# Two-block kernel: recurrent results kept on chip, adaLN in 1024-column steps, five taps on other engines, channel norm between tiles

## The reference

```python
h = rmsnorm(x, norm_g) * (1 + scale) + shift
cv, cg, cs, lx, ls = split(h @ w_in)                  # 5 x 1024 channels
v = cv * sigmoid(cg)
v = causal_depthwise_conv(v, dw_w, dw_b)              # 31 taps
v = silu(layernorm(v, cln_g, cln_b))                  # over channels
y_conv = (v @ pw2_w + pw2_b) * silu(cs)
xs = causal_depthwise_conv(lx, sc_w, sc_b)            # 4 taps
r, i = sigmoid(xs @ wr + br), sigmoid(xs @ wi + bi)   # 8 heads of 128
a = exp(-8 * r * softplus(-lam))
hs = linear_scan(a, sqrt(1 - a * a) * i * xs)         # along tokens
y_lru = hs * silu(ls)
x = x + (1 + gate) * (concat(y_conv, y_lru) @ w_out); x = rmsnorm(x, final_g)
# second block
mods_x, mods_ctx = silu(c_2) @ ada_w + ada_b, silu(c_ctx) @ ada_w + ada_b
# mLSTM mixer in both directions over a context of 256 and the 1024 tokens, then a gated conv-FFN
```

## Time and profile before

| | us |
|---|---|
| median of 3 runs | 2440.98 |
| the three runs | 2440.98, 2437.72, 2441.24 |
| the profiled execution, its own time | 2437.03 |
| its span in the trace | 2435.2 |
| TensorE matmul busy | 2170.7 (89%) |
| DVE busy | 1205.0 (49%) |
| ACT busy | 722.6 (30%) |
| POOL busy | 660.5 (27%) |

### The profile page before, as it was taken

The page is one execution under the profiler, slowest core; times in us unless marked ns, Lnnn a source line. Parts: engine busy times, 40 slices in busy tenths (PEclk is TensorE's granted clock), DMA queues, the critical chain, the costliest instruction groups (busy, mean ns, idle before and its releaser), DMA issues.

```text
span 2435.2 us, 25833 instructions
## 1 busy us (share of the span) xinstructions
PE 2170.7 (89%) x9824; PEld 1791.3 (74%) x9824; DVE 1205.0 (49%) x1196; ACT 722.6 (30%) x827; POOL 660.5 (27%) x300
## 2 busy tenths in 40 slices
PE   3599999995889997999997994978999999999995
PEld 3488777774667775788886993846888888887874
DVE  6699989998563436603305654045222222222124
...
GB/s 302 152 52 52 37 117 97 117 72 62 113 52 69 121 78 18 162 81 201 214 100 259 225 157 233 43 95 27 51 43 69 78 64 65 78 61 113 74 56 69
DMA packets 290235, 251.43 MB, mean 103 GB/s; under 512 B 7091, under 2 KB 262676, under 8 KB 290164
## 3 DMA queue, kind: packets, MB, share of 16 engines
...
## 4 chain that ended last, share of the span: by engine, by line
PE 51%; issue 32%; POOL 6%; DVE 5%; DMA 4%; ACT 2%; SPq 0%; ACTq 0%; POOLq 0%; DVEq 0%
PE PS L1277 40%; POOL wl L667 4%; PE PS L1519 1%; PE PS L1511 1%; PE PS L1512 1%; DVE SCR L1623 1%; PE PS L1545 1%; PE PS L1397 1%; PE PS L1299 1%; DMA B<-rows_d 1%; DMA B<-in_mod_w 1%; DMA SCR<-lru_d 1%; PE PS L1485 1%; PE PS L1505 1%; DMA SCR<-in_ctx 1%
## 5 line engine op out<-in xcount | busy, mean ns | idle before, releaser
L1277 PE MATMUL PS<-XH,wh 128*128 128x512 f32 x2416 | 753.0, 393 | 34.3 <-POOL wl L667 25.2
L1277 PE MATMUL PS<-XH,wl 128*128 128x512 f32 x2416 | 748.7, 391 | 0.0
L1277 PE MATMUL PS<-XL,wh 128*128 128x512 f32 x2416 | 748.6, 391 | 0.0
L667 POOL TENSOR_TENSOR wl<-raw,wh 128x1024 fp32r<-128x1024 f32 (+2 forms) x173 | 409.0, 2364 | 1214.0 <-ACT wh L851 1044.4
L1277 PEld LDWEIGHTS PS<-XH,wh 128*128 128x128 f32 x2416 | 454.5, 189 | 135.1 <-issue 19.8
L1277 PEld LDWEIGHTS PS<-XH,wl 128*128 128x128 f32 x2416 | 456.7, 189 | 96.2
L1277 PEld LDWEIGHTS PS<-XL,wh 128*128 128x128 f32 x2416 | 456.2, 189 | 95.7
L1709 DVE SCALAR_TENSOR_TENSOR PS<-B,PJ,PS 128x1022 f32<-128x1022 f32 (+28 forms) x232 | 295.1, 1272 | 8.2 <-DVE SC L1765 0.2
L851 ACT ACTIVATE wh<-raw 128x1024 fp32r<-128x1024 f32 (+1 forms) x124 | 129.5, 1045 | 309.2 <-PE PS L1277 223.1
L2073 DVE SCALAR_TENSOR_TENSOR SCR<-SCR,PV 128x1008 f32<-128x1008 f32 x22 | 28.0, 1271 | 256.6 <-ACT SCR L1213 256.6
L914 ACT ACTIVATE wh<-raw 128x1024 fp32r<-128x1024 f32 (+1 forms) x48 | 45.6, 950 | 237.0 <-PE PS L1277 205.1
(11 more groups left out here) (304 smaller groups left out, 2440.6 us busy)
## 6 DMA issues: line engine op xcount, KB each, us to landing
...
```

Source lines behind the costliest of these rows:

```text
L667: tt(wl[slot][:, 0:kc, :], raw[slot][:, 0:kc, :], wh[slot][:, 0:kc, :].bitcast(F32), ALU.subtract).then_inc(lo_done, 1)
L1277: last = mm(ps[:, c:c + step_n], W[:, k, :], Y[:, k, c:c + step_n], start=(seen == 0), stop=(seen == total - 1))
```

## The change

Recurrent results: step i writes its product to a buffer of its own (`lru_out[i]`), and nothing goes to DRAM or back. After its last taps DVE splits the first five, high and low, then forms the eighth; ACT rounds the last three, DVE subtracts for all. The output product is one of eight tiles (G1). Its first two tiles run in the order: tile one chunks 1 to 7, tile two chunks 1 to 4, tile one chunk 8, tile two chunks 5 to 8. In the eighth step the gate product stands before the cs tile, and ACT makes the filter's high part before it empties ls. The cs tile frees the input's chunks one by one.

adaLN: 16 + 32 row tiles of 128 x 1024 are loaded one by one, the early ones in three buffers, behind the weight loads of the convolution's tiles. DVE adds two accumulators in turn, all before the first tap. TensorE sums them after the convolution's seventh and eleventh tile. The late ones stand three per tile beside the projection.

Taps: for seven of the eight chunks five taps leave DVE's list. ACT starts a side sum with one tap and the bias and multiplies four more, POOL adds them, and DVE's tap 1 takes the side sum in. The list has 27 steps for these chunks and 32 for the last; 100 stand ahead of the recurrent steps.

Norm: mean, variance and reciprocal root stand before G1's tiles four, seven and eight. ACT squares, DVE adds. G2's first tile takes its chunks as they come, its second follows.

```diff
+    SIDE = 5
...
-        ada_t = b2[:, 0:3 * D].rearrange("p (k n) -> p k n", k=KD)
...
+        ada_t = [b2[:, n * D:(n + 1) * D] for n in (3, 6, 7)]
+        late_t = [b2[:, n * D:(n + 1) * D] for n in range(4)]
+        EARLY, LATE = 2, 4
+        ada_acc = [(T[0], T[3]), (T[1], T[6])]
+        side_t = [b2[:, n * D:(n + 1) * D] for n in range(3)] + [T[5]] + [b2[:, n * D:(n + 1) * D] for n in range(3)]
+        side_tmp = (T[4], T[2])
+        late_acc = b1[:, 2 * ALL:2 * ALL + LATE * D]
+        lru_out = [b2[:, n * D:(n + 1) * D] for n in (4, 5, 0, 1, 2)] + [T[0], T[1], T[3]]
...
-        STEPS = TAPS + 1
-        AHEAD = KD // 2
-        SHARE = [11 if i < EARLY else 17 for i in range(KD)]
-        CONV_AT = [AHEAD * STEPS + sum(SHARE[:i]) for i in range(KD + 1)]
+        STEPS = TAPS - SIDE + 1
+        AHEAD = 100
+        SHARE = [17] * (KD - 2) + [13, (KD - 1) * STEPS + TAPS + 1 - AHEAD - 17 * (KD - 2) - 13]
+        CONV_AT = [AHEAD + sum(SHARE[:i]) for i in range(KD + 1)]
...
-            return 2 * KD + 4 * i + 2
+            return 2 * KD + 4 * i + (2 if i < KD - 1 else 3)
 
         def gate_unit(i):
-            return 2 * KD + 4 * i + 3
...
-            def ada_load(h):
-                if h:
-                    sp.wait_ge(*at("ada_summed", h))
-                sp.dma_start(ada_t, ada_w.rearrange("(k p) n -> p k n", p=P)[:, :, HALF * h:HALF * (h + 1)]).then_inc(ev("ada_in"), 16)
-
-            def y_store(i):
-                sp.wait_ge(*at("lru_y", i + 1))
-                sp.dma_start(lru_d[P * i:P * (i + 1), :], r_t).then_inc(ev("lru_out"), 16)
+            def ada_load(n):
+                if n >= 3:
+                    sp.wait_ge(*at("ada_summed", 2 * (n - 2)))
+                h, k = divmod(n, KD)
+                sp.dma_start(ada_t[n % 3], ada_w[P * k:P * (k + 1), D * h:D * (h + 1)]).then_inc(ev(f"ada_in{n % 3}"), 16)
...
+            for n in range(3):
+                ada_load(n)
+            for U in range(4, 2 * KD):
+                l1_load(U)
+                for n in range(3 * (U - 3), min(3 * (U - 2), EARLY * KD)):
+                    ada_load(n)
...
-                sp.dma_start(lru_t[k % 2], lru_d[k * P:(k + 1) * P, :]).then_inc(ev(f"lru_in{k % 2}"), 16)
...
+            def side_add(j, m):
+                n, d = (SIDE - 1) * j + m, TAPS - SIDE + 1 + m
+                pool.wait_ge(*at("side_tmp", n + 1))
+                if m == 0:
+                    pool.wait_ge(*at("side_init", 2 * (j + 1)))
+                else:
+                    pool.wait_ge(*at("side_sum", n))
+                s = side_t[j][:, d:SEQ]
+                tt(s, s, side_tmp[m % 2][:, 0:SEQ - d], ALU.add).then_inc(ev("side_sum"), 1)
...
             for j in range(KD):
                 l1_low(cg_unit(j) + 2)
+                if j:
+                    side_add(j - 1, 0)
+                    side_add(j - 1, 1)
...
-                if i in (0, 1, 4, 7):
-                    conv_sum({0: 2, 1: 3, 4: 4, 7: 5}[i])
...
+                if i in (0, 1, 3, 4, 6):
+                    conv_sum({0: 2, 1: 3, 3: 4, 4: 5, 6: 6}[i])
+            l1_low(cs_unit(KD - 1) + 2)
...
+            def side_mult(j, m):
+                n, d = (SIDE - 1) * j + m, TAPS - SIDE + 1 + m
+                if n >= 2:
+                    act.wait_ge(*at("side_sum", n - 1))
+                f(side_tmp[m % 2][:, 0:SEQ - d], B1[:, j, 0:SEQ - d], ACT.Copy, scale=PJ[:, j, TAPS - 1 - d:TAPS - d]).then_inc(ev("side_tmp"), 1)
+
+            def side_init(j):
+                d, bias = TAPS - SIDE, PJ[:, j, TAPS:TAPS + 1]
+                act.wait_ge(*at("v_ok", j + 1))
+                if j >= 4:
+                    act.wait_ge(*at("side_read", j - 3))
+                f(side_t[j][:, 0:d], bias.to_broadcast([P, d]), ACT.Copy).then_inc(ev("side_init"), 1)
+                f(side_t[j][:, d:SEQ], B1[:, j, 0:SEQ - d], ACT.Identity, scale=PJ[:, j, TAPS - 1 - d:TAPS - d], bias=bias).then_inc(ev("side_init"), 1)
...
+            for i in range(KD):
+                last = i == KD - 1
+                if last:
+                    xs_high(i)
+                    ls_evac(i)
+                else:
+                    ls_evac(i)
+                    xs_high(i)
+                    hi(cs_unit(i) + 2)
+                    cs_evac(i)
...
+            cs_evac(KD - 1)
+            hi(cs_unit(KD - 1) + 2)
+            for k in range(DVE_HIGH, KD):
+                lru_high(k)
...
+            squares = {2: (0, 3), 3: (3, KD - 1), 4: (KD - 1, KD)}
+            for t in range(KD - 1):
+                g1_evac(t)
+                for k in range(*squares.get(t, (0, 0))):
+                    ln_square(k)
+                if t == KD - 3:
+                    act.wait_ge(*at("var_ps", 1))
+                    f(small[:, 1, 0:NT], PS[3][:, 0:NT], ACT.Sqrt, bias=eps[:]).then_inc(ev("ln_sd"), 1)
...
+                if i < KD - 1:
+                    tile(cs_unit(i), 0, PS[1], taken[1], KD + 2 * i + 1)
+                    gates(i)
...
+                    gates(i)
+                    tile(cs_unit(i), 1, PS[1], taken[1], KD + 2 * i + 1, release="x_used_L1")
...
+            def late_chunk_opening(g, ready):
+
+                for s, k0, k1 in ((0, 0, KD - 1), (1, 0, KD // 2), (0, KD - 1, KD), (1, KD // 2, KD)):
+                    w, ps = (g.U + s) % 2, PS[(g.T + s) % 2]
+                    if k0 == 0:
+                        pe.wait_ge(lo_done, g.U + s + 3)
+                        pe.wait_ge(taken[(g.T + s) % 2], (g.T + s) // 2 + 1)
+                    for k in range(k0, k1):
+                        pe.wait_ge(*at(ready, k + 1))
+                        for n, (W, Y) in enumerate(((wh[w], XH), (wl[w], XH), (wh[w], XL))):
+                            for c in range(0, SEQ, 512):
+                                last = mm(ps[:, c:c + 512], W[:, k, :], Y[:, k, c:c + 512], start=(k == 0 and n == 0), stop=(k == KD - 1 and n == 2))
+                    if k1 == KD:
+                        last.then_inc(unit_used, 1)
+
+            late_chunk_opening(G1, "xl_G1")
+            for t in range(2, KD):
+                if t == 3:
+                    pe.wait_ge(*at("msum_ok", KD))
+                    pe.wait_ge(*at("r_ok", KD))
+                    stat(PS[2], msum_t, event="mean_ps")
+                elif t == KD - 2:
+                    pe.wait_ge(*at("ln_sum", KD - 1))
+                    token_sums(PS[3], T[5], event="var_ps")
+                elif t == KD - 1:
+                    pe.wait_ge(*at("ln_diag", 1))
+                    stat(PS[3], T[6], event="ln_r")
+                b = (G1.T + t) % 2
+                tile(G1.U + t, (G1.U + t) % 2, PS[b], taken[b], (G1.T + t) // 2, release="x_used_G1" if t == KD - 1 else None)
...
+            for h in range(EARLY):
+                ada_sum(h)
             conv_steps(0, CONV_AT[0])
+            dve.wait_ge(*at("ada_used", EARLY))
+            V.tensor_copy(ADA[:, 0:EARLY * KD, :], PS[2][:, 0:2 * EARLY * KD].rearrange("p (c t) -> p c t", t=2)).then_inc(ev("ada_sb"), 1)
             for i in range(KD):
                 short_conv(i)
                 if i:
                     lru(i - 1)
-                if 1 <= i <= EARLY:
-                    ada_copy(i - 1)
-                if i < EARLY:
-                    ada_sum(i)
...
+            for k in range(DVE_HIGH):
+                g1_high(k)
+                g1_low(k)
             lru(KD - 1)
-
-
...
             for k in range(KD):
-                step.link(V.tensor_tensor(B1[:, k, :], B1[:, k, :], PS[2][:], ALU.subtract))
-                if k == 0:
-                    step.link(V.tensor_tensor(T[5], B1[:, 0, :], B1[:, 0, :], ALU.mult))
-                else:
-                    step.link(V.tensor_tensor(T[4], B1[:, k, :], B1[:, k, :], ALU.mult))
-                    step.link(V.tensor_tensor(T[5], T[5], T[4], ALU.add))
-            dve.sem_inc(ev("var_ok"), 1)
+                V.tensor_tensor(B1[:, k, :], B1[:, k, :], PS[2][:], ALU.subtract).then_inc(ev("ln_sub"), 1)
+            for k in range(1, KD):
+                dve.wait_ge(*at("ln_sq", k + 1))
+                if k >= 2:
+                    dve.wait_ge(*at("ln_sum", k - 1))
+                V.tensor_tensor(T[5], T[5], sq_t[(k - 1) % len(sq_t)], ALU.add).then_inc(ev("ln_sum"), 1)
```

304 lines of the change are left out of this document (157 added, 147 removed).

## The result

The changed kernel took 2416.06 us (median of 4 runs, 2414.37 to 2417.37), beside 2439.35 us for the kernel before. The ratio is 0.9904, with a 95% interval of 0.9887 to 0.9921: some 23 us faster, where 34 were forecast. The time lies in the stated range (2378 to 2422), near its upper end, outside the forecast case's own 2394 to 2412, and near the second rival's 2419. A later measurement of both on another occasion gave 0.9923 (0.9906 to 0.9939).

A forecast was written before the change was run, and what follows sets the result against it. TensorE was taken as the bound except for waits in the recurrent steps, the turn and the channel norm. Gains of 16.3 and 28.0 less losses of 9.8 and 0.6 made 33.9 us off 2437.03: 2403 us, range 2378 to 2422.

The forecast's parts named there:

- forecast case: The prediction's own main case for the whole kernel: 2394 to 2412 us, chance 0.60.
- second rival: Early adaLN: row loads delay the taps past about 166 us, DVE is late to the first filter; 2419 us, chance 0.15.
- (a): adaLN products moved ahead of the recurrent steps: taps start at 161 us, six periods take 224.6 us, gain 16.3 us.
- (c): Five taps off DVE in the convolution's tiles, using ACT and GpSimd: costs nothing, saves DVE 45 us.
- (b): adaLN column sums on TensorE: two runs of 16 among the convolution's tiles lose 9.8 us, late ones 0.6 us.
- (d): Eighth step, gate product ahead of cs: TensorE idles 10 us, gates at g+32.9; part of a joint 28.0 us gain.
- (e): Turn into the output product: chunk 6 ready at g+68, third tile near g+84; part of a joint 28.0 us gain.
- g: Time origin for the last step and turn: the end of the seventh step's gate product, 547.9 us before the change.
- (f): Channel norm between output tiles without idle: 95.8 us, next product's third tile at g+179.8; part of a joint 28.0 us gain.
- GpSimd as the bound of the tiles: Rival in the convolution's tiles: GpSimd operations at 4.0 us each cost 43 us over seven pairs; 2446 us, chance 0.03.
- The covers hold: Rival: GpSimd avoids scans, gates wait 5 us, chunk 6 near g+59, all six periods 36.3 us; 2383 us, chance 0.22.
- The idle is only moved: Within the main case, 0.60: 31 us of TensorE idle become 10 at the gates, about 10 in the turn.

The follow-up runs named there:

- accumulation in PSUM: Changed kernel with DVE's 32 early adaLN products accumulating in PSUM instead of SBUF; 2407.0 us, ratio 0.9877 to the kernel before.
- the run with the norm after the tiles: Changed kernel with variance and reciprocal root behind the output product's last tile, the mean still between tiles; 2433.26 us, ratio 0.9987 to the kernel before.

## Why the prediction was right or wrong

- **(a) failed in one sentence: "At a tap's price of 1.28 us they are 41 us of DVE."** They took 73.9. The contention had been priced some paragraphs earlier from the earlier trace rows held the 384-column product at 1.139 us beside GpSimd and 0.619 without. But the price was taken from taps that read PSUM, while the products were to read and write SBUF, in the one stretch where part (c) gave GpSimd 16.8 us of work in 21.8. With the price's condition restored (accumulation in PSUM) the predicted 161 us came out as 161.83, and DVE was in time for the first filter by 8.2 us, where 5 were forecast. Of the step's own sums, 17 tiles of 10.9 us back from 304.26 give 119, not 116, and 161 and 100 steps of 1.27 give 288, not 287; the third tile started at 115.06 before and at 116.36 now, so the 152 and the 161 built on it were not hurt.
- The rest of (a) held. Two periods of 36.3 were measured as 36.28 and 36.31, the four of 38.0 as 39.4, 39.7, 38.1 and 38.4. The first two are longer by TensorE's clock, 0.96 for 1.00; with PSUM they are 38.0 and 38.1. A fall of the clock within a step was no term of the sum. Before, it had cost some 1.6 us in each of the periods four to six, by the same reading (granted clock 0.96 in each).
- **(b) was undersized**, 13.6 for 9.8. The price of a sum came from short runs and from a long one whose own clock fell; the 2.2 us that the following tile loses were left to the rounding of a bound. The cost also varies: one of two runs of sums stayed near the forecast in the run with the norm after the tiles (3.6 us).
- **(c)** held for TensorE's tiles (no gain there when the additions go) and failed in what stands beside them.
- **(d), (e)** held in the path: idle 9.54 for 10, gates at g+31.9 for 32.9, scan's last input at g+54.0 for 54.7, chunk 6 at g+64.6 for 68, third tile at g+81.8 for 84 (68, 15.0 and 2.4 add up to 85.4; measured, 17.2 us lie between the two). Chunk 6 came near the place of the other rule, sharing (g+65.5), but not by it: the five pairs of the split ended at g+55.8 and not at g+60. Behind them the rows show turns, as assumed. Scan and product, 3.5 us alone, and the two GpSimd operations beside them, 4.8 alone, take 8.7 us together (609.35 to 618.07). What the prediction didn't ask is whether the new order of the eighth step pays: undone, it is 3 us faster by the timeline.
- **(f)** held: 95.8 us from third tile to third tile, as counted, with waits of 0.19 to 0.84 us in between, and 14.4 us are lost when two of the three statistics lose their cover.
- **The rivals.** "DVE comes late to the first filter" happened, by its condition (taps after 166 us, measured 187), but at a chance of 0.15 and with a wrong reason: not the row loads but the products' price. Nor did the lateness carry into the steps: DVE was in time from the second on. It cost 4.46 us of idle, some 1.3 us in the tiles ahead and, counting both falls of the clock, 3.0 in the periods, about 9 for 16. That the time stands near this rival's 2419 is chance, a sum of other things: the 9 us, the 4 us by which (b) was short, and the 2 us that (d) to (f) gave more. GpSimd as the bound of the tiles didn't come: it took 2.4 to 2.8 us an operation up to 151 us and 3.1 to 3.4 from there to 185, with one of 3.18 at 117.66, and TensorE waited for it 0.5 us more at the third tile (2.81 for 2.30) and nowhere behind it. "The covers hold" didn't come either: the gates waited 9.54 us, four of six periods were 38 or more, and the scan was blocked. (Its first gain, 11 us, isn't worked out; g+68 to g+59 is 9.) "The idle is only moved" did: 30.93 us became 9.54 at the gates and 8.75 in the turn. Of the signs of being wrong, "periods near 40 us" came for two of the six.
- **Left open**: what keeping the results on chip alone brings, and the splits of chunks 1 to 5 on DVE alone; neither was tried apart from the rest. Nor is it known what decides whether TensorE's clock falls within a step.
